# One-pass LayerNorms, four memory projections at each of four of them, and an output projection opened on seven heads

## The chip, the core and the metric

The kernel is one program on one core of a Trainium2 chip. It has a TensorE (PE, with PEld for its weight loads), a VectorE (DVE), a ScalarE (ACT), a GpSimd (POOL) and a SyncE (SP), which issues transfers. The metric is the device time of one execution in microseconds (us), as the median of several runs of the same kernel. Lower is better.

## What is computed

A two-layer decoder trunk is applied to 512 prompt tokens and to 32 sample tokens (8 sequences of 4), width 1024, all in float32. Each layer is a mixer, an attention over 256 memory tokens and a feed-forward part, and each of these three is added to the scaled stream and normalised:

```python
def _layer_norm(x, g, b):
    mu = jnp.mean(xf, axis=-1, keepdims=True)
    var = jnp.mean(jnp.square(xf - mu), axis=-1, keepdims=True)
    return ((xf - mu) * lax.rsqrt(var + LN_EPS) * g + b).astype(x.dtype)

for i in range(DEPTH):
    # layer 0: RG-LRU mixer; layer 1: gated delta rule
    x = _layer_norm(DN_ALPHA * x + mix, ...)                               # 0 and 3
    x = _layer_norm(DN_ALPHA * x + _mem_attention(x, mk, mv, wq, wo), ...) # 1 and 4
    # layer 0: SwiGLU; layer 1: 8 experts, 2 of them per token
    x = _layer_norm(DN_ALPHA * x + ff, ...)                                # 2 and 5
```

The numbers behind the lines are those by which the kernel counts its LayerNorms. The keys and values of the memory, `mem_prompt` times `xa_wk` and `xa_wv` of both layers, are outputs too; the sample tokens attend to cached ones. The delta rule has 8 heads of 128; each head's output is normalised by its root mean square, gated, and then all go through one output projection.

## The kernel before

**Layout.** Activations lie feature by feature: `x` is 128 partitions by 8 tiles (KT) by 544 tokens. A feature sum across partitions is therefore a product with a matrix of ones. For projections in front of the experts, each operand is split into a high and a low part (`xh` and `xl`, `wh` and `wl`), and a tile of output is 48 matmuls: high times high, low weight times high, high weight times low, 8 feature tiles and 2 halves of 272 tokens each (`lin_steps`, L537).

**Weights.** SP loads slots of 512 KB into a ring of 4 (`raw`, L389 to L437). POOL splits each into `wh` (L467) and `wl` (L471), each in four pieces. These have 2 places, so that POOL may split a slot only when the slot two before it has been used. PE reports a used slot on `w_used`, with the last of its 48 products. The 16 memory projections of each layer (`kv`, L584) need no split: they read `raw` and a copy of the memory `A_mem`; tiles 0 to 7 are keys (L600), 8 to 15 values (L604). Those of layer 1 are done within the LayerNorms 0 to 2, by `KV1_AT` (L23): 2 and 2 in the first, 3 and 5 in the second, 2 and 2 in the third. Their slots stand in the order of the slots between those of the projections on both sides. Layer 1's keys and values are stored to memory and loaded again after the delta rule, which uses the same place.

**A LayerNorm** (PE L567, ACT L1165, DVE L1641). While the projection before it runs, DVE evicts each tile (`residual`, L1659; L1666) and adds it to a running sum (L1656). Behind the last tile PE sums that over features (L570), DVE subtracts the mean from all eight tiles (L1644), ACT squares each of them (L1172) into one of two buffers, PE sums these over tiles and features (L577), ACT makes the reciprocal deviation (Ln L1177, Exp L1178), DVE multiplies eight tiles (L1647), ACT writes the eight high parts (L1182) and then the eight results (L1186), and DVE the low parts (L1633). The first part of the memory projections stands on PE's queue behind the first sum, the second behind the last one; ACT evicts each (L1141 to L1145), the second part between the results. In front of LayerNorm 2, DVE adds up the eight tiles only after the last of them (L1725).

**What follows each.** 0 and 3: the query projection of the attention (`linear`, L560), its first tile in the order of the feature tiles as they become ready; 1: the feed-forward part (`experts`, L692); 2: the delta rule's projections, begun with 30 products, then a small projection for its rates (L810); 4: the router (L1022), with three token transposes after its fourth feature tile (L1014), and then the routing. LayerNorm 5 is computed token by token in the branch taken here (L1147); `layer_norm(5)` is the other branch's.

**The end of the delta rule.** Head 7's output is evicted (`out_parts`), squared by ACT (L1413), summed by PE (`out_length`, L857, which waits for the sample state's `d_ssn`, L1909), scaled and gated (`out_norm`), and split into `hh` and `hl`. PE then waits for the eighth head's low part (L999), and the output projection, 8 tiles of 48, begins. ACT loads the keys and values back and fetches the first three pieces of cached keys (L1199) behind the last tile.

## Time and profile before

| | us |
|---|---|
| median of 3 runs | 2652.28 |
| lowest and highest run | 2652.21, 2659.44 |
| the profiled execution, its own time | 2667.02 |
| its span, first to last instruction | 2665.0 |

| engine | busy us | share of the span | instructions |
|---|---|---|---|
| PE | 2407.8 | 90% | 17290 |
| PEld | 2284.6 | 86% | 17290 |
| POOL | 961.3 | 36% | 1397 |
| DVE | 854.4 | 32% | 1423 |
| ACT | 536.4 | 20% | 1017 |

The mean granted TensorE clock of that execution is 0.931 of full speed. Busy time is an average over stages with different limits: a PE that is busy for 90% of the span still has gaps, and those are found by stage, with the chain of waits and the windows.

### The profile page before, as it was taken

What the parts mean: (1) busy time and instruction counts of PE and PEld (TensorE: products, weight loads), DVE (VectorE), ACT (ScalarE), POOL (GpSimd) and SP (SyncE); (2) the same over time, 40 slices, a digit from 0 to 9 for tenths busy, and PEclk for the clock granted to TensorE, in tenths of its full rate; (3) what the DMA queues carried; (4) which work ended last, traced back from release to release, by engine and by line L of the source; (5) the groups of instructions that cost most, each with busy time, mean ns of one, the idle gap of its engine ahead of it and who ended that gap; (6) DMA issues with size and microseconds to landing.
All of it is one profiled execution on the core that took longest, in us unless ns stands there. A gap on an engine that the chain in (4) does not pass through costs nothing.

```text
span 2665.0 us, 42930 instructions
## 1 busy us (share of the span) xinstructions
PE 2407.8 (90%) x17290; PEld 2284.6 (86%) x17290; DVE 854.4 (32%) x1423; ACT 536.4 (20%) x1017; POOL 961.3 (36%) x1397
## 2 busy tenths in 40 slices
PE   8998889999999987999999888889689999999993
PEld 8988858899999967899989777777579999999993
DVE  3673222211011037666666542412301000000004
ACT  2450320310011033333322211321200000100103
POOL 4546614588888725433322103544100000000001
PEclk9999999999999988999988777899789999999996
DMA  7314341322222221211111101341255677788884
GB/s 285 99 61 177 126 182 59 115 88 79 88 87 87 79 71 59 58 59 59 58 52 59 35 25 64 148 160 64 79 188 180 220 238 238 232 266 268 279 286 161
DMA packets 98376, 347.55 MB, mean 130 GB/s; under 512 B 13488, under 2 KB 18736, under 8 KB 93344
## 3 DMA queue, kind: packets, MB, share of 16 engines
q1 hardware_dynamic: 73136, 279.08, 31.2%
q10 hardware_dynamic: 19056, 44.65, 4.7%
q0 software_dynamic: 6016, 21.43, 2.2%
q8 instruction: 122, 2.00, 0.3%
q14 instruction: 46, 0.38, 0.0%
HBM read 318.66 MB, written 26.47 MB: 130 GB/s over the span
## 4 chain that ended last, share of the span: by engine, by line
PE 73%; DVE 10%; issue 7%; DMA 4%; ACT 3%; POOL 2%; ACTq 0%; DVEq 0%; SPq 0%; POOLq 0%
PE ps L548 29%; PE ps L1073 14%; PE ps L1088 8%; PE ps L727 6%; DMA raw<-weights 2%; PE ps L600 2%; PE ps L577 2%; PE ps L604 1%; PE ps L936 1%; PE ps L638 1%; PE ps L932 1%; DVE x L1647 1%; PE ps L915 1%; POOL wl L471 1%; PE ps L774 1%
## 5 line engine op out<-in xcount | busy, mean ns | idle before, releaser
L467 POOL TENSOR_TENSOR wh<-raw,tab 128x256 fp32r<-128x256 f32 x672 | 425.5, 664 | 940.7 <-PE ps L548 744.2
L471 POOL TENSOR_TENSOR wl<-raw,wh 128x256 fp32r<-128x256 f32 x672 | 507.3, 785 | 0.0
L1073 PE MATMUL ps<-work,raw 128*128 128x128 f32 (+6 forms) x3072 | 424.8, 300 | 13.4 <-DMA raw<-weights 11.0
L1073 PEld LDWEIGHTS ps<-work,raw 128*128 128x128 f32 x3072 | 420.5, 191 | 16.3 <-DVE work L2112 6.8
L548 PE MATMUL ps<-xh,wh 128*128 128x272 f32 x2048 | 309.8, 304 | 41.4 <-ACT work L1353 10.6
L548 PEld LDWEIGHTS ps<-xh,wh 128*128 128x128 f32 x2048 | 282.4, 199 | 50.8 <-issue 18.2
L548 PE MATMUL ps<-xh,wl 128*128 128x272 f32 x2048 | 296.8, 295 | 0.0
L548 PE MATMUL ps<-xl,wh 128*128 128x272 f32 x2048 | 281.8, 288 | 1.5 <-DVE xl L1633 1.4
L548 PEld LDWEIGHTS ps<-xh,wl 128*128 128x128 f32 x2048 | 275.3, 193 | 1.8 <-issue 0.5
L548 PEld LDWEIGHTS ps<-xl,wh 128*128 128x128 f32 x2048 | 265.5, 188 | 2.6 <-DVE xl L1633 2.6
L517 POOL DMA_DIRECT2D rows_y<-moe_h x8 | 4.3, 538 | 656.9 <-DVE moe_h L2105 656.9
L1088 PE MATMUL ps<-work,raw 128*128 128x128 f32 (+6 forms) x1536 | 218.0, 298 | 0.8 <-DVE work L2112 0.8
L1088 PEld LDWEIGHTS ps<-work,raw 128*128 128x128 f32 x1536 | 209.6, 190 | 1.6 <-DVE work L2112 1.4
L2112 DVE TENSOR_TENSOR work<-moe_h,ps 128x128 f32<-128x128 f32 (+6 forms) x96 | 30.6, 319 | 440.1 <-ACT moe_h L1563 440.1
L1563 ACT ACTIVATE moe_h<-ps 128x128 f32<-128x128 f32 (+6 forms) x96 | 29.0, 302 | 396.4 <-PE ps L1073 396.3
L1713 DVE TENSOR_TENSOR work<-work,ps 128x544 f32<-128x544 f32 x24 | 17.3, 721 | 225.8 <-PE ps L548 225.8
L2105 DVE COPY moe_h<-ps 128x256 f32<-128x256 f32 (+1 forms) x64 | 25.1, 391 | 197.2 <-PE ps L1061 155.6
L727 PE MATMUL ps<-hh,wh 128*128 128x272 f32 x384 | 81.4, 294 | 6.7 <-DVE hl L1633 6.7
L727 PE MATMUL ps<-hh,wl 128*128 128x272 f32 x384 | 80.4, 292 | 0.0
L727 PE MATMUL ps<-hl,wh 128*128 128x272 f32 x384 | 80.4, 292 | 0.0
L1172 ACT ACTIVATE lnsq<-x 128x544 f32<-128x544 f32 x40 | 26.3, 657 | 210.0 <-DVE x L1644 195.0
L1666 DVE SCALAR_TENSOR_TENSOR x<-x,ps 128x544 f32<-128x544 f32 x32 | 23.1, 721 | 139.9 <-PE ps L548 139.9
(358 smaller groups left out, 3121.3 us busy)
## 6 DMA issues: line engine op xcount, KB each, us to landing
raw<-weights SPq DMA_DIRECT2D x488, 512.0 KB, 3.9
moe_h<-cache SPq DMA_DIRECT2D x6, 2048.0 KB, 8.9
moe_h<-cache ACTq DMA_DIRECT2D x4, 2048.0 KB, 13.6
work<-cache SPq DMA_DIRECT2D x4, 2048.0 KB, 8.9
moe_h<-rows_x POOLq DMA_DIRECT2D x14, 512.0 KB, 7.8
rows_x<-lnsq ACTq DMA_DIRECT2D x9, 512.0 KB, 11.0
work<-scratch ACTq DMA_DIRECT2D x16, 272.0 KB, 4.2
work<-cache ACTq DMA_DIRECT2D x2, 2048.0 KB, 10.4
```

Source lines behind the costliest of these rows:

```text
L467: nc.gpsimd.tensor_tensor(flat(h1[:, k0:k1]), flat(r1[:, k0:k1]), one_col, MUL).then_inc(pool_hi, 1)
L471: low = nc.gpsimd.tensor_tensor(flat(l1[:, k0:k1]), flat(r1[:, k0:k1]), flat(h1[:, k0:k1]).bitcast(F), SUB)
L548: last = mm(ps[:, 2 * i + h, 0:HT], w[:, par_, k, :], a[:, k, h * HT:(h + 1) * HT], start=(n == 0 and k == 0), stop=(n == 2 and k == KT - 1))
L577: last = mm(ps[:, 6 + h, 0:HT], ones, lnsq[:, k % 2, h * HT:(h + 1) * HT], start=(k == 0), stop=(k == KT - 1))
L600: last = mm(ps[:, b, 0:MEM], raw[:, q, k, :], A_mem[:, k, :], start=(k == 0), stop=(k == KT - 1))
L604: last = mm(ps[:, b, mt * P:(mt + 1) * P], A_mem[:, k, mt * P:(mt + 1) * P], raw[:, q, k, :], start=(k == 0), stop=(k == KT - 1))
L638: last = mm(ps[:, 4 + tt // 2, (tt % 2) * MEM:(tt % 2 + 1) * MEM], A_q[:, 2 * h + kk, tt * P:(tt + 1) * P], A_k[:, 2 * h + kk, :], start=( ...
L727: last = mm(ps[:, 2 * d + h, 0:HT], w[:, s % 2, k, :], a[:, f, h * HT:(h + 1) * HT], start=(f == 0 and m == 0), stop=(f == FT - 1 and m == 2))
L1073: last = mm(ps[:, j // 2, (j % 2) * c:(j % 2 + 1) * c], raw[:, slot % RAW, k, :], M_x[:, r % 2, k, 0:c], start=(k == 0), stop=(k == KT - 1))
L1088: last = mm(ps[:, 2 + d % 2, 0:c], raw[:, slot % RAW, k, :], M_h[:, f, 0:c], start=(f == 0), stop=(f == FT - 1))
L1563: s(A(M_s[:, f % 2, 0:c], ps[:, f % 2, 0:c], ACT.Silu), m_silu, e12 + f + 1)
L2112: s(V.tensor_tensor(M_h[:, f, 0:c], M_s[:, f % 2, 0:c], ps[:, f % 2, c:2 * c], MUL), m_h, e12 + f + 1)
```

## The change

The LayerNorms 0 to 4 take the mean of the squares in place of the mean of squared differences. While a projection runs, ACT squares each evicted tile (`squares`) and DVE adds the square to a second running sum (`add_square`). Behind the last tile there are two sums over features, one next to the other; the variance is the second less the square of the first (`z_mean`), clipped at 0. DVE centres tile 0 before the variance and tile 1 after it, the other six each in front of its product with the deviation.

`KV1_AT` gives each of the LayerNorms 0 to 3 four projections of layer 1: one before the two sums, three behind them. ACT evicts the first behind the square of the mean and the others behind the first three high parts. The memory is loaded a second time for the last four, and of the values only the first half is loaded back. The first pieces of cached keys are fetched behind LayerNorms 0 and 3 instead of ahead of them.

Behind the LayerNorms 0, 1 and 3 PE does the high-part products of the first two tiles before the low-part products of either. In the output projection `opening` does all three parts of the first two tiles for the heads 0 to 6, and then the head 7 for both. The eighth head's sums no longer wait for the sample state and have other banks. The router's transposes stand behind its sixth feature tile instead of its fourth. In front of LayerNorm 2 the additions stand between the evictions. `layer_norm(5)` keeps its old form as `last_norm`.

```diff
-KV1_AT = {0: (0, 2, 4), 1: (4, 7, 12), 2: (12, 14, 16)}
+KV1_AT = {0: (0, 4), 1: (4, 8), 2: (8, 12), 3: (12, 16)}
...
             def linear(slot, direct, ah, al, freed, base, fresh=None, opened=False):
+                if fresh is not None:
+                    pairs = [lin_steps(slot + s, direct, s, s, ah, al, fresh=fresh, per=2 * KT) for s in range(2)]
+                    for steps in pairs:
+                        next(steps)
+                        next(steps)
+                    for steps in pairs:
+                        for _ in steps:
+                            pass
...
             def layer_norm(n):
+                if n in KV1_AT:
+                    lo, hi = KV1_AT[n]
...
+                    kv(1, lo, lo + 1)
+                pe.wait_ge(z_sum, n + 1)
+                for h in range(2):
+                    last = mm(ps[:, 6 + h, 0:HT], ones, lnsq[:, 0, h * HT:(h + 1) * HT], start=True, stop=True)
+                last.then_inc(ln_sum, 1)
+                pe.wait_ge(z_sq, n + 1)
+                for h in range(2):
+                    last = mm(ps[:, 4 + h, 0:HT], ones, lnsq[:, 1, h * HT:(h + 1) * HT], start=True, stop=True)
+                last.then_inc(ln_var, 1)
+                if n in KV1_AT:
+                    kv(1, lo + 1, hi)
+                    pe.wait_ge(kv_ev, 16 + hi)
...
+            def squares(n):
+                act.preload_act_table_set("natural_log_exp_and_others")
+                for t in range(KT):
...
+                    if t >= 2:
+                        act.wait_ge(z_acc, (KT - 2) * n + t - 1)
+                    s(A(lnr[:, :] if t else lnsq[:, 1, :], x[:, t, :], ACT.Square), z_pw, KT * n + t + 1)
...
             def layer_norm(n):
-                lo, mid, hi = KV1_AT[n] if n in KV1_AT else (0, 0, 0)
+                lo, hi = KV1_AT[n] if n in KV1_AT else (0, 0)
+                act.wait_ge(ln_sum, n + 1)
+                s(A(two(lnsq[:, 0, :]), pair(3), ACT.Square, scale=D ** -0.5), z_mean, n + 1)
+                if lo < hi:
+                    kv(1, lo)
+                act.wait_ge(z_var, n + 1)
+                s(A(lnr[:, :], lnr[:, :], ACT.Ln, bias=pc("eps5"), scale=1.0 / D))
+                s(A(lnr[:, :], lnr[:, :], ACT.Exp, scale=-0.5), ln_std, n + 1)
...
+                for k in range(KT):
+                    upper(n, k)
+                    if lo + 1 + k < hi:
+                        kv(1, lo + 1 + k)
+                for k in range(KT):
+                    result(n, k)
...
             def layer_norm(n):
+                dve.wait_ge(z_mean, n + 1)
+                centre(0)
+                dve.wait_ge(ln_var, n + 1)
+                s(V.tensor_tensor(two(lnr[:, :]), pair(2), two(lnsq[:, 0, :]), SUB))
+                s(V.tensor_scalar(lnr[:, :], lnr[:, :], 0.0, None, ALU.max), z_var, n + 1)
+                centre(1)
+                dve.wait_ge(ln_std, n + 1)
+                for k in range(KT):
+                    if k >= 2:
+                        centre(k)
+                    s(V.tensor_tensor(x[:, k, :], x[:, k, :], lnr[:, :], MUL), ln_n, n * KT + k + 1)
...
+            def add_square(t, n):
+                if t:
+                    dve.wait_ge(z_pw, KT * n + t + 1)
+                    add = V.tensor_tensor(lnsq[:, 1, :], lnsq[:, 1, :], lnr[:, :], ADD)
+                    s(add, *((z_acc, (KT - 2) * n + t) if t < KT - 1 else (z_sq, n + 1)))
...
             out_length(GH - 1)
-            pe.wait_ge(d_yl, GH)
             pe.wait_ge(d_z, GH)
-            linear(S_GOUT, 32, hh, hl, z_ready, KT * 2)
+            opening(S_GOUT, 28, hh, hl, range(GH - 1), (d_yh, d_yl))
+            linear(S_GOUT, 28, hh, hl, z_ready, KT * 2, opened=True)
```

## Rows read from the trace of the kernel before

**Rows 1.** The page: the chain that ended last, by line.

```profile
PE ps L548 29%; PE ps L1073 14%; PE ps L1088 8%; PE ps L727 6%; DMA raw<-weights 2%; PE ps L600 2%; PE ps L577 2%; PE ps L604 1%; PE ps L936 1%; PE ps L638 1%; PE ps L932 1%; DVE x L1647 1%; PE ps L915 1%; POOL wl L471 1%; PE ps L774 1%
```

**Rows 2.** The chain of waits, LayerNorm 0: start us, us, what.

```profile
261.33 1.19 PE ps L570 x4
262.52 6.91 PE ps L600 x32
269.42 7.88 PE ps L577 x32
...
277.39 0.72 ACT lnr L1177
...
278.13 0.67 ACT lnr L1178
...
287.74 0.85 ACT xh L1182
...
290.77 0.39 ACT work L1141
...
291.21 8.81 PE ps L548 x52
```

**Rows 3.** Windows, five LayerNorms: PE, PEld, DVE, ACT, POOL; clock, DMA share, GB/s.

```profile
259.70:291.20 31.50, 22.87 (x100) 18.42 (x100) 16.83 (x20) 17.86 (x26) 13.45 (x16) 0.96 0.61 234
454.60:500.00 45.40, 39.28 (x230) 34.64 (x229) 17.33 (x23) 20.90 (x32) 10.77 (x15) 0.96 0.25 82
946.10:984.40 38.30, 25.93 (x165) 23.00 (x164) 19.52 (x26) 16.57 (x25) 10.09 (x16) 0.88 0.25 82
1685.50:1704.00 18.50, 11.65 (x36) 8.00 (x36) 9.21 (x13) 8.77 (x13) 5.54 (x8) 0.82 0.97 395
1874.40:1890.20 15.80, 9.32 (x37) 6.18 (x37) 8.88 (x13) 7.48 (x12) 0.00 (x0) 0.99 0.00 0
```

**Rows 4.** Timeline, ends of five stages: start us, us, engine, line, operation.

```profile
305.67 2.33 POOL L467 TENSOR_TENSOR wh<-raw,tab 128x256 fp32r<-128x256 f32 x4 [0.90 <-PE ps L548]
...
512.13 2.18 PE L548 MATMUL ps<-xh,wh 128*128 128x272 f32 x16
...
990.27 7.51 PE L810 MATMUL ps<-x,par 128*8 128x272 f32 x64
...
1724.34 2.18 PE L548 MATMUL ps<-xh,wh 128*128 128x272 f32 x16
...
1908.94 0.19 DVE L2059 COPY work<-ps 128x32 f32<-128x32 f32 x1 [14.42 <-PE ps L1022]
```

**Rows 5.** Line L1656, additions: duration ns min/median/max.

```profile
L1656 DVE TENSOR_TENSOR lnsq<-lnsq,x x30: 724/986/1052, 230.2 to 1875.2; 128x544 f32<-128x544 f32 x30
```

**Rows 6.** Timeline: POOL's splits; output tiles 2 and 7.

```profile
299.67 2.33 POOL L467 TENSOR_TENSOR wh<-raw,tab 128x256 fp32r<-128x256 f32 x4 [12.61 <-PE ps L548]
301.95 2.81 POOL L471 TENSOR_TENSOR wl<-raw,wh 128x256 fp32r<-128x256 f32 x4
...
1647.64 2.23 PE L548 MATMUL ps<-hh,wh 128*128 128x272 f32 x16
...
1653.95 3.29 POOL L467 TENSOR_TENSOR wh<-raw,tab 128x256 fp32r<-128x256 f32 x4
...
1679.25 2.24 PE L548 MATMUL ps<-hh,wh 128*128 128x272 f32 x16 [0.27 <-POOL wl L471]
```

**Rows 7.** Timeline and window behind a gap of 2.55 us.

```profile
404.63 3.65 PE L548 MATMUL ps<-xh,wh 128*128 128x272 f32 x16 [2.55 <-issue]
...
404.60:408.00 3.40, 3.37 (x16) 3.40 (x17) 0.00 (x0) 0.00 (x0) 0.00 (x0) 0.56 0.00 0
```

**Rows 8.** Timeline: a value projection of the memory.

```profile
479.15 3.73 PE L604 MATMUL ps<-raw,work 128*128 128x128 f32 x32
```

**Rows 9.** Timeline: the sums for head 7's norm.

```profile
1624.76 2.15 PE L862 MATMUL ps<-lnsq,tab 128*128 128x272 f32 x4 [3.88 <-DVE work L1909]
```

**Rows 10.** Transfers: count, KB each, median us to landing.

```profile
moe_h<-cache ACTq DMA_DIRECT2D x4, 2048.0 KB, 13.6
```

More of the change, by code:

```diff
@@ L1723, in one @@
                           f_y, e8 + (d + 1))
-                repeat(dve, n, one, s)
-                for k in range(KT):
-                    add_tile(k, n_ln)
+                        if isinstance(e, int) and e + 1 == n:
+                            add_tile(d, n_ln)
+                            add_square(d, n_ln)
+                if gated:
+                    repeat(dve, n, one, s)
+                else:
+                    for e in range(n):
+                        one(e)
             def log1p_half(e, t0, t1, t2):
```

199 lines of the change are left out of this document (130 added, 69 removed).

## The prediction

> **What bounds the kernel now.** I read the page's chain by line first: its large shares are PE's products (L548 29%, L1073 14%, L1088 8%), a transfer holds 2% [rows 1]. Time is won where PE stands still, not by faster engines elsewhere. Next came the chain of waits around LayerNorm 0, for the order in which its steps end [rows 2]: the sum over features (1.19), two memory projections (6.91), a ping-pong of squares and their sums (7.88), Ln and Exp (0.72, 0.67), a DVE and ACT phase; the next projection starts at 291.21. PE's last product ended at 259.70, so the stage takes 31.5 us. Then the windows, one per LayerNorm, each from PE's last product to its next dense work [rows 3]: POOL is idle for more than half of every one. LayerNorm 5 lies in a branch that this input doesn't take (the chain runs through L1073 and L1088, in the other one [rows 1]).
>
> Last came the points where a stage really ends. POOL splits weights two slots ahead of PE, so a stage is over when the third tile behind it (tile 2) starts. Now that is, for LayerNorm 0, 305.6 (POOL's split at 305.67 waits for the same product), 45.9 after PE's last one; for 1: 512.13, 57.5; for 3: 1724.34, 38.8. Stage 2 ends with the small beta/rate projection, 990.27 + 7.51 = 997.8, 51.7; stage 4 with the logits copied out at 1908.94, 34.5 [rows 4].
>
> **The new LayerNorm, from PE's last product at 0.** A DVE step on a tile takes 0.72 and 0.03 to issue [rows 5]. DVE evicts tile 7 and adds it to the sum (0.1 + 2 x 0.72), ACT squares it beside that (0.67), DVE adds the square (0.72): sums complete at 1.6 and 2.4. In stages 0 to 3 one projection stands first in PE's queue (6.91 / 2 = 3.45), so the two cross-feature sums end at 4.6 and 5.6. ACT squares the mean (0.72): 5.4. DVE centres tile 0 (0.75), subtracts (0.72), clips. The trace has no such clip: at least half an addition, 0.36, at most a whole one, 0.72; I take 0.43. With Ln and Exp the reciprocal deviation is there at 8.9, against 278.8 - 259.7 = 19.1 now [rows 2].
>
> Part of that goes back, since six of eight centrings now stand behind the deviation. Additions of two tiles take 0.72 alone and up to 1.05 [rows 5], the latter while POOL splits, as it will here; a product with the deviation has the same form. 2 x 1.05, then 6 x (0.75 + 1.05 + 0.04) puts the last one at 22.1; high part 23.0 (0.85 and 0.02 each), eight results 30.0, last low part 30.8. The three other projections end with their evictions near 16 and hide under this; uncovered they would cost 3 x 3.45. PE's products of high parts trickle behind ACT until 23.3; then low weights 2.6, the second tile's 32 products 4.3, both tiles' low parts 4.4: 34.6. The two open tiles hold both slots, the first until 32.4. Only then can POOL start slot 2, 2.33 + 2.81 [rows 6]: tile 2 at 37.7.
>
> So PE waits 3.1 us, and that has its own price: behind 2.55 us without work the granted clock was 0.56, mostly the 1.2 GHz level, and 16 products took 3.65 [rows 7] against 2.18 in [rows 4]. With what the next 16 lose I count 1.65.
>
> Stage **0**: 45.9 - 37.7 - 1.65 = 6.5 won. **1**: four of its eight projections go to stage 3: 57.5 - 37.7 - 1.65 = 18.1 won. **2**: DVE no longer adds eight tiles behind the last eviction; projections are 3.73 each [rows 8] and PE waits 0.9 for tile 7 first; deviation at 9.9, high parts 24.0, 14 products at the low clock 2.9, the small projection 7.5: 34.7 instead of 51.7, 17.0 won. **3** takes up four projections (14.9) and can load weights only as they free slots; they end near 19 and still hide: 38.0 instead of 38.8, less the wait: 0.8 lost. **4**, without projections: deviation at 7.1, first result at 8.8 instead of 15.8; PE's router products and turns follow as now: 7.0 won.
>
> **The output projection.** Its first two tiles may start on seven heads once the sums for the eighth's norm are out. PE now waits 3.88 for them (until 1624.76, for the sample state's L1909) and they run at the low clock, four in 2.15 where [rows 2] has 1.19 [rows 9]. Without that wait they start near 1622.7. Behind them 42 products, the first 16 cold, 7.1; 42 more, 5.7; the eighth head. The first slot is free at 1638.5, and with a split of 5.65 tile 2 starts at 1644.1 instead of 1647.64 [rows 6]: 3.5, of which 1.5 goes for the cold start behind this new gap. At full clock it would be 5.6 in all, and 0 if the eighth norm were late; I take 2.0.
>
> **What the sums cost on the way.** Every evicted tile brings DVE one more addition with both operands in SBUF while POOL splits. Two of them stretch four POOL pieces from 2.33 to 3.29 [rows 6], 0.48 each. POOL's slot goes from 5.6 to 6.1 in three projections and from 6.1 to 6.6 in the fourth; PE's tile takes 6.0 (299.67 to 305.67). The fourth shows what 6.1 does: six tiles 6.32 apart, 1647.64 to 1679.25. So 18 x 0.27 = 4.9, and 6 x 0.28 = 1.7, 6.6 lost. Bounds: 0 if the additions fall where POOL idles; above, the first rival. In the feed-forward's down phase (under 0.7 per slot) POOL's idle 0.90 [rows 4] covers them; without it some 0.6 per slot.
>
> The queues: SP loads the same 488 slots, POOL skips the unsplit ones as now. ACT fetches 4 MB (layer 0) and 6 MB (layer 1) of cached keys after the LayerNorm instead of before, and reloads the memory (1 MB) beside the keys at the end of head 7, some 45 us before PE wants it. I cost these at 0: they land under eight query tiles of 6 us; uncovered, the last rival but one. ACT's new waits (each square for the addition before it) hold back nothing due, and DVE's wait for the square only the next eviction, due 6 us later.
>
> **Sum**: 6.5 + 18.1 + 17.0 - 0.8 + 7.0 + 2.0 - 6.6 = 43.2. The profiled execution lasted 2667.0 (span 2665.0 and 2.0 around it), 14.7 over the median; it would become 2624, and the median 2652.3 - 43.2 = 2609, which I predict.
>
> **Rivals.**
> *POOL becomes the bound of the projections.* In [rows 5, 6] both sides lose part of an addition (0.33, 0.48). If each addition stopped POOL for its whole 0.72, slots would be 6.6 in three projections and 7.3 in the fourth: 18 x 0.6 + 6 x 1.0 = 17 lost instead of 6.6: 2619. The Trainium skill (SBUF — State Buffer, "Who interferes with whom") states that rule: the later of two such operations blocks fully. By that rule this case should hold everywhere; the rows show less. 15%.
>
> *Evictions queue behind the high parts.* PE may not open before the last projection is evicted, and just such an eviction (0.39 at 290.77) released it at 291.21 [rows 2]. If the last comes behind the eighth high part instead of the third, PE begins 7 us later, cold, and does in a burst what would have trickled: 3 per stage, 12 in all: 2621. Against: 16 is well under 23. 10%.
>
> *No price for short waits.* Gaps that cost no clock and additions that fall into POOL's idle time: 3 x 1.65 + 1.5 + 6.6 = 13 more, 2596. Against: the 2.55 us row. 15%.
>
> *Slower: cached keys arrive late.* In layer 1 three fetches of 2 MB start some 31 us behind PE's last product instead of at once; the scores want them at about 80. ACT's fetches now land in 13.6 us [rows 10], three in a row 41, under the 49 there are. Above 16 us each PE stands; from (49 + 43) / 3 = 31 us each the gain is gone; at 36 the kernel takes 2668. For it: weights share the queues. Against: beside LayerNorm 3 the fetches moved at 395 GB/s [rows 3]. 4%.
>
> *It doesn't do what it says*: the shorter chains end in the same wait for POOL or low parts, and stages 1 and 2 keep half of their gain: 17.6 less, 2627. 4%.
>
> **How the numbers follow.** Forecast (2600 to 2618) 52%, the rivals as said. 2590 to 2626 leaves out the last two (8%) and the tails of the others; it takes in 0 to 17 for POOL, 0 to 5.6 for the opening, 0 to 6 for the gaps. 0.3% (8 us) is about what a measurement can tell from no change: faster than that in all but the slower case and some far tails: 0.93; same 0.03; slower 0.04.
>
> **What would show it.** Right: two groups of four sum products per LayerNorm; Ln some 7.5 us behind PE's last product (17.7 now); POOL's third split at 32 to 33, tile 2 at 37 to 40 in stages 0, 1 and 3; logits out near 27.5 in stage 4; six output tiles 6.6 apart. Wrong: tile 2 past 42, POOL's slots past 6.6, PE waiting for the cache, the small projection ending past 38. A result above 2644 would mean that the stages end elsewhere than I read them.

## The result and the profile after

The changed kernel takes 2637.25 us (2634.41 to 2642.49, 6 runs) where the kernel before takes 2659.20 (2652.21 to 2664.01) on the same chip: ratio 0.9912, 95% interval 0.9893 to 0.9932. A second series gave 2635.79 and 0.9901 (0.9884 to 0.9918). So it is faster, by 22 to 27 us, where 43.2 were forecast; the forecast ratio of 0.9836 (2609 over 2652.3) lies outside both intervals. The two profiled executions differ by as much: a span of 2639.3 now, 2665.0 before.

The page's chain by line still has PE's products in front ([rows 1]), but POOL's splits (L472, L468) now make up 5% of it, where the page before gives POOL 2%:

```profile
PE ps L550 25%; PE ps L1138 14%; PE ps L1153 8%; PE ps L788 4%; POOL wl L472 3%; DMA raw<-weights 3%; POOL wh L468 2%; PE ps L651 1%; DVE x L1762 1%; PE ps L1000 1%; PE ps L996 1%; PE ps L979 1%; PE ps L655 1%; PE ps L835 1%; DVE x L1750 1%
```

Stage by stage, from the two traces (PE's last product is the end of the projection ahead of a LayerNorm, or the start of the memory projection that now follows it at once, 0.16 us before that end; LOUT, O and GOUT are the recurrence's, the attention's and the delta rule's output projections):

| stretch | before | after | won | forecast |
|---|---|---|---|---|
| everything up to LOUT's first product | 208.8 | 206.9 | 1.9 | 0 |
| LayerNorm 0: last product to the scores of attention 0 | 82.6 | 85.0 | -2.4 | +6.5 |
| scores and outputs of attentions 0 and 1 | 125.1 | 129.5 | -4.4 | 0 |
| LOUT and O, O: first product to last | 151.0 | 154.0 | -3.0 | -4.9 |
| LayerNorm 1: last product to the first down phase | 193.5 | 178.2 | 15.3 | 18.1 |
| first down phase and second up phase | 224.5 | 222.9 | 1.5 | 0 |
| second down phase | 73.5 | 76.3 | -2.8 | 0 |
| LayerNorm 2: last product to the small projection's end | 51.7 | 35.5 | 16.2 | 17.0 |
| from there to GOUT's last product | 687.7 | 688.7 | -1.0 | +0.3 |
| LayerNorm 3: last product to the scores of attention 1 | 76.0 | 78.5 | -2.5 | -0.8 |
| LayerNorm 4: last product to the logits | 34.6 | 27.7 | 6.9 | 7.0 |
| from the logits to the end | 756.1 | 756.1 | 0 | 0 |
| sum | | | 25.7 | 43.2 |

In the column of what was won, a minus is time lost. The new LayerNorm does what its steps said. Here is PE behind LOUT, which ends at 258.10 (timeline of PE; start us, us, engine, line, operation, in brackets the idle time before and who ended it). [Rows 2] has the same stage before:

```profile
261.55 1.08 PE L613 MATMUL ps<-lnsq,tab 128*128 128x272 f32 x4
262.46 1.08 PE L617 MATMUL ps<-lnsq,tab 128*128 128x272 f32 x4
...
280.68 0.82 PE L550 MATMUL ps<-xh,wh 128*128 128x272 f32 x2 [0.69 <-ACT xh L1244]
281.30 3.80 PE L550 MATMUL ps<-xh,wl 128*128 128x272 f32 x16
...
288.95 4.16 PE L550 MATMUL ps<-xl,wh 128*128 128x272 f32 x32
303.88 3.99 PE L550 MATMUL ps<-xh,wh 128*128 128x272 f32 x16 [10.77 <-ACT work L1300]
```

The cross-feature sums end 4.5 and 5.4 us behind the last product (4.6 and 5.6 forecast), the eighth high part is there at 22.5 (23.0), and POOL's third split runs from 291.26 to 296.3, 33.2 to 38.2 behind (32.4 to 37.7). But the third query tile starts at 303.88, 45.8 behind instead of 37.7, after 10.77 us in which PE waited for ACT's line L1300, the eviction of query tile 0. The chain of waits says why (start us, us, what):

```profile
258.26 3.45 PE ps L651 x16
...
288.60 14.58 DMA out_mem_k<-work
...
303.88 38.49 PE ps L550 x288
```

ACT had issued two fetches of 2 MB of cached keys, then the store of four projected keys to `mem_k`, and then waited for that store, because the buffer `A_st` shares its bytes with the attention's `A_pt` (`act.wait_ge(out_done, 80)` ahead of `attention(0)`). The view of the transfers to `out_mem_k` has it with its price:

```profile
L1426 ACTq DMA_DIRECT2D out_mem_k<-work x1: 488/488/488, 288.6 to 288.6; - x1
...
  ACT work L1300: 15.6, 1
...
DMA to landing us min/median/max: 14.6/14.6/14.6
```

The two fetches landed 7.6 and 12.9 us behind their issue, the second at 301.0, and the store 2.2 us behind that (transfers of line L1295):

```profile
DMA to landing us min/median/max: 7.6/10.3/12.9
```

Before, ACT issued the fetches ahead of the LayerNorm; they had landed by 273.4 when the same store went out at 296.4, and it landed in 2.7 us (transfers to `out_mem_k` in the kernel before):

```profile
DMA to landing us min/median/max: 2.7/2.7/2.7
```

In the window in which it was under way now, 366 GB/s were moved, and PE's granted clock was 0.73 on average:

```profile
288.60:303.20 14.60, 4.51 (x37) 4.29 (x35) 1.76 (x1) 0.00 (x0) 10.07 (x16) 0.73 0.98 366
```

The other stages end as forecast, a little late. These lines answer to [rows 4] (timeline): the third tile of the feed-forward's first up phase, of the query projection behind LayerNorm 3, and the copy of the logits:

```profile
497.68 4.00 PE L550 MATMUL ps<-xh,wh 128*128 128x272 f32 x16 [3.75 <-POOL wl L472]
...
1698.82 3.96 PE L550 MATMUL ps<-xh,wh 128*128 128x272 f32 x16 [3.35 <-POOL wl L472]
...
1883.18 0.19 DVE L2197 COPY work<-ps 128x32 f32<-128x32 f32 x1 [9.86 <-PE ps L1086]
```

The third tiles start 39.2 and 38.9 us behind PE's last product (37.7 and 38.0 forecast), logits are out at 27.7 (27.5). Both tiles run cold, which in this text means at the lower of the clock's two levels, 1.2 GHz: the granted clock (the third number from the end) is 0.50 in the window of the first, as in that of the second.

```profile
497.68:501.68 4.00, 4.00 (x17) 4.00 (x18) 0.00 (x0) 0.00 (x0) 4.00 (x7) 0.50 0.41 131
```

### The profile page after: what moved, and what is told of

It is laid out like the page before. It is cut to its first block, busy times and chain, and to the rows that moved or that the text cites. A ratio compares the mean times of both kernels' runs of the same rounds, so it can differ in the third digit from the quotient of the medians.

```text
span 2639.3 us, 42728 instructions
## 1 busy us (share of the span) xinstructions
PE 2380.0 (90%) x17150; PEld 2264.9 (86%) x17150; DVE 898.8 (34%) x1468; ACT 540.3 (20%) x1022; POOL 985.0 (37%) x1397
## 4 chain that ended last, share of the span: by engine, by line
PE 63%; issue 15%; DVE 10%; POOL 5%; DMA 4%; ACT 3%; ACTq 0%; POOLq 0%; DVEq 0%; SPq 0%
PE ps L550 25%; PE ps L1138 14%; PE ps L1153 8%; PE ps L788 4%; POOL wl L472 3%; DMA raw<-weights 3%; POOL wh L468 2%; PE ps L651 1%; DVE x L1762 1%; PE ps L1000 1%; PE ps L996 1%; PE ps L979 1%; PE ps L655 1%; PE ps L835 1%; DVE x L1750 1%
## 5 line engine op out<-in xcount | busy, mean ns | idle before, releaser
L468 POOL TENSOR_TENSOR wh<-raw,tab 128x256 fp32r<-128x256 f32 x672 | 438.8, 684 | 898.0 <-PE ps L550 603.1
L472 POOL TENSOR_TENSOR wl<-raw,wh 128x256 fp32r<-128x256 f32 x672 | 518.6, 803 | 0.0
L1138 PE MATMUL ps<-work,raw 128*128 128x128 f32 (+6 forms) x3072 | 424.2, 299 | 13.2 <-DMA raw<-weights 10.8
L550 PEld LDWEIGHTS ps<-xh,wh 128*128 128x128 f32 x2048 | 284.3, 200 | 70.0 <-issue 20.8
L550 PE MATMUL ps<-xh,wl 128*128 128x272 f32 x2048 | 303.5, 299 | 0.0
L550 PEld LDWEIGHTS ps<-xh,wl 128*128 128x128 f32 x2048 | 281.7, 198 | 1.8 <-issue 0.5
L788 PEld LDWEIGHTS ps<-hh,wh 128*128 128x128 f32 x384 | 61.5, 193 | 8.7 <-issue 8.3
L1240 ACT ACTIVATE lnr<-x 128x544 f32<-128x544 f32 x35 | 23.1, 660 | 214.7 <-DVE x L1798 157.7
```

The costliest lines, as they stand in the source:

```text
L468: nc.gpsimd.tensor_tensor(flat(h1[:, k0:k1]), flat(r1[:, k0:k1]), one_col, MUL).then_inc(pool_hi, 1)
L472: low = nc.gpsimd.tensor_tensor(flat(l1[:, k0:k1]), flat(r1[:, k0:k1]), flat(h1[:, k0:k1]).bitcast(F), SUB)
L550: last = mm(ps[:, 2 * i + h, 0:HT], w[:, par_, k, :], a[:, k, h * HT:(h + 1) * HT], start=(n == 0 and k == 0), stop=(n == 2 and k == KT - 1))
L788: last = mm(ps[:, 2 * d + h, 0:HT], w[:, s % 2, k, :], a[:, f, h * HT:(h + 1) * HT], start=(f == 0 and m == 0), stop=(f == FT - 1 and m == 2))
L1138: last = mm(ps[:, j // 2, (j % 2) * c:(j % 2 + 1) * c], raw[:, slot % RAW, k, :], M_x[:, r % 2, k, 0:c], start=(k == 0), stop=(k == KT - 1))
```

## The experiments

All ratios are to the kernel before on the same chip.

**The store first.** In ACT's program:

```diff
+            act.dma_start(O["mem_k"][1][:, 0:4, :], A_st).then_inc(out_done, 16)
             act.wait_ge(w_used, S_LOUT + 8)
             piece(0, 1)
             piece(0, 2)
-            act.dma_start(O["mem_k"][1][:, 0:4, :], A_st).then_inc(out_done, 16)
             act.wait_ge(out_done, 80)
```

> The changed kernel with one move: behind LayerNorm 0, ACT issues the 0.5 MB store of four projected keys before the two 2 MB fetches of cached keys, not after them. Theory (the store waited behind 4 MB that the same queue had just been given): it lands in about 3 us instead of 14.58, ACT evicts query tile 0 at once, and the third query tile starts 38 us behind PE's last product, with POOL's third split, instead of 45.8: about 7.5 us won against the changed kernel, some 2630 us, ratio to before near 0.989. Rival (memory traffic of weights and keys slows any store at that place): it still takes over 10 us, the third tile starts past 43, no time is won. Second rival (the fetches, issued some 0.5 us later, then come late for the scores): PE waits several us more for cached keys near the fourth head (now 0.28) and gives the gain back there.

Measured: 2634.31 us, ratio 0.9892 (0.9877 to 0.9907). The store landed in 3.6 us, PE's wait is for POOL again, and the stretch from LOUT's last product to the scores is 77.65 us instead of 85.03 (transfers to `out_mem_k`, then PE's timeline):

```profile
DMA to landing us min/median/max: 3.6/3.6/3.6
...
298.45 3.58 PE L550 MATMUL ps<-xh,wh 128*128 128x272 f32 x16 [3.33 <-POOL wl L472]
```

The cached keys hardly came late: PE's wait for them in attention 0 is 0.7 us (0.3 in the changed kernel). The intervals of the two ratios (0.9892 here, 0.9912 for the change) overlap; that the stage is 7.4 us shorter is read from the traces.

**One fetch ahead of the store.** The store between `piece(0, 1)` and `piece(0, 2)`:

> The changed kernel with the same store between the two 2 MB fetches: one ahead of it, not two. Theory (it waits for the bytes ahead of it in ACT's queue): it lands in roughly half of 14.58, 7 to 9 us, near 296 us of the span, about when POOL has split the third weight slot (296.3), so PE's wait for ACT shrinks from 10.8 to 3 to 4 us, of which POOL's split is the end. Rival (memory traffic): near 14 us as with two ahead. Rival (a fixed price for any store behind any fetch): near 14 us too.

Measured (one run, 2627.39 us, beside 2663.73): the store landed in 10.5 us, PE waited 6.02 for ACT and the third tile started at 299.72.

```profile
DMA to landing us min/median/max: 10.5/10.5/10.5
...
299.72 3.59 PE L550 MATMUL ps<-xh,wh 128*128 128x272 f32 x16 [6.02 <-ACT work L1300]
```

So 3.6, 10.5 and 14.6 us with none, one and two fetches ahead of it (13.4 for two in a second run of the change): each 2 MB adds to the wait, the first more than the second, so that 10.5 is over the expected 7 to 9. The fetch ahead of the store explains the size: it landed in 8.3 us (the lowest value of its line), and the store 2.6 us behind it, about the 2.7 that the store takes alone.

```profile
DMA to landing us min/median/max: 8.3/11.9/15.6
```

Neither rival (14 us whatever stands ahead, or no change with the store first) survives. The Trainium skill (DMA: Bandwidth & Descriptors, "Queues, rings and completion order") says that each transfer engine consumes the descriptors of a ring in order and that a transfer's semaphore is raised only after the earlier writes of the same transfer engine; the three landings agree with that.

**One tile first.** The change interleaves the two first tiles of a projection behind a LayerNorm, as in the prediction. Here they run one after the other, in `linear` and in the experts' `up`:

```diff
-                if fresh is not None:
-                    pairs = [lin_steps(slot + s, direct, s, s, ah, al, fresh=fresh, per=2 * KT) for s in range(2)]
...
-                for s in range(2 if opened or fresh is not None else 0, 8):
+                for s in range(2 if opened else 0, 8):
...
-                    lin_tile(slot + s, direct, s % 2, s % 2, ah, al)
+                    lin_tile(slot + s, direct, s % 2, s % 2, ah, al, fresh=fresh if s == 0 else None)
```

> As the run with the store first, and in the three projections that follow LayerNorms 0, 1 and 3 the two first tiles are not interleaved: tile 0 runs through its three parts as the LayerNorm delivers them, then tile 1. Theory (POOL's third split waits for tile 0's slot, which the interleaving holds until tile 1's low weights are through): the slot is free when the last low part is (about 30.5 us behind PE's last product instead of 33.2), POOL's third split ends near 35.7, PE runs tile 1 (6 to 8 us) meanwhile and has no gap, and the third tile starts at 36.7 to 38.5 with PE at its high clock instead of at 38.2 to 39.1 at the low one: 1.5 to 4 us won in each of three stages, 4 to 12 in all against the run with the store first. Rival (the interleaving is what pays for the early start: without it 32 products of tile 1 that were hidden stand on the path): third tile at 40 or later, slower by 2 to 4 us per stage, 6 to 12 in all.

Measured: 2611.98 us, ratio 0.9805 (0.9790 to 0.9821). PE behind LOUT, whose last product ended at 259.4:

```profile
282.60 3.83 PE L550 MATMUL ps<-xh,wl 128*128 128x272 f32 x16
286.23 2.45 PE L550 MATMUL ps<-xl,wh 128*128 128x272 f32 x12
...
290.16 2.16 PE L550 MATMUL ps<-xh,wh 128*128 128x272 f32 x16
...
296.16 2.16 PE L550 MATMUL ps<-xh,wh 128*128 128x272 f32 x16
```

Tile 0 is done at 290.2, tile 1 runs without a stop while POOL splits, and the third tile starts at 296.16, 36.8 behind the last product, with no idle time and at 2.16 us for 16 products. The stretches to the scores or the down phase are 4.0, 4.8 and 3.8 us shorter than with the store first, at LayerNorms 0, 1 and 3. That is 12.5 of the 22 us between the two medians. Of the 20.8 us between the two profiled spans, 10.8 lie behind the logits, where nothing was changed (761.9 and 751.1 us): see "chance" below. The interleaving does not pay: the products that it does early are ones for which there is time anyway, since POOL cannot split before a slot is free.

**One tile first in the output projection.** `opening` finishes tile 0 (seven heads, then the eighth) before it starts tile 1:

```diff
-                    for n, (w, a) in enumerate(parts):
-                        for k in tiles:
...
-                rest = range(tiles[-1] + 1, KT)
-                for s in range(2):
-                    for n, (w, a) in enumerate(parts):
-                        for k in rest:
...
+                    for ks in (tiles, range(tiles[-1] + 1, KT)):
+                        for n, (w, a) in enumerate(parts):
+                            for k in ks:
```

> As the run with the store first, and the delta rule's output projection opens one tile after the other: tile 0 with seven heads and then with the eighth, only then tile 1, instead of both tiles with seven heads and then both with the eighth. Theory (opening both at once holds both weight slots, so that POOL's third split starts only at 1612.7 while the eighth head's low part had been there since 1606.4): POOL starts near 1607.5, the third tile near 1613.2 without PE's idle 6.45 and without the cold 16 products (3.64 instead of 2.18): 7 to 8 us won there, of which some goes back where POOL's slots stay 6.1 to 6.6 apart: 5 to 8 us against the run with the store first. Rival (the projection is bound by POOL's pace of 6.5 behind the opening whatever its start): under 2 us.

Measured: 2622.92 us, ratio 0.9836 (0.9822 to 0.9850). In the changed kernel (timeline of PE, then of POOL) the projection opens 1.6 us behind the sums at 1598.23, and POOL's third split waits until both tiles are through; the third tile starts 20.0 us behind the opening, after 6.45 idle:

```profile
1598.23 2.18 PE L926 MATMUL ps<-lnsq,tab 128*128 128x272 f32 x4 [2.06 <-ACT lnsq L1511]
1599.83 3.33 PE L570 MATMUL ps<-hh,wh 128*128 128x272 f32 x14
...
1619.85 3.64 PE L550 MATMUL ps<-hh,wh 128*128 128x272 f32 x16 [6.45 <-POOL wl L472]
...
1612.72 2.81 POOL L468 TENSOR_TENSOR wh<-raw,tab 128x256 fp32r<-128x256 f32 x4 [134.68 <-PE ps L579]
1615.49 4.21 POOL L472 TENSOR_TENSOR wl<-raw,wh 128x256 fp32r<-128x256 f32 x4
```

With tile 0 first (POOL's timeline, then PE's) the split starts 7.7 us behind the opening at 1594.17, the third tile 13.4 behind it, without a gap:

```profile
1601.84 2.81 POOL L468 TENSOR_TENSOR wh<-raw,tab 128x256 fp32r<-128x256 f32 x4 [129.46 <-PE ps L571]
...
1607.59 2.23 PE L550 MATMUL ps<-hh,wh 128*128 128x272 f32 x16
```

GOUT takes 56.1 us from its first product to the sums of LayerNorm 3, against 63.6 (7.5 won, at the top of the expected 5 to 8). The medians differ by 11.4 from the run with the store first, more than this stage gives.

**No opening.** PE waits for the eighth head's low part and then runs tile after tile:

```diff
-            opening(S_GOUT, 28, hh, hl, range(GH - 1), (d_yh, d_yl))
-            linear(S_GOUT, 28, hh, hl, z_ready, KT * 2, opened=True)
+            pe.wait_ge(d_yl, GH)
+            pe.wait_ge(d_ssn, GH)
+            linear(S_GOUT, 28, hh, hl, z_ready, KT * 2)
```

> The run with the store first, without the opening with seven heads: the delta rule's output projection starts when the eighth head's low part is there (about 8.2 us behind the sums for its norm), tile after tile, as before the change. Theory (both opened tiles held both slots, so the opening as it is won little): tile 0 starts near 8.3 us behind the sums' first product, cold, 8.2 us long, slot 0 is free at 16.5, POOL's third split ends at 22.2 and the third tile starts at 22.6 with PE at its high clock, against 21.6 with the opening, cold behind its gap of 6.45 (1.5 lost there): within 1 us of the run with the store first, slower or faster. Rival (the opening is worth the 2 us forecast or more): third tile 2 us or more later than with it after counting the cold start, 2 to 3.5 us slower.

Measured: 2627.86 us, ratio 0.9868 (0.9853 to 0.9884), no slower than with the opening. Tile 0 starts 8.3 behind the sums, the third tile 23.15, and from the sums to the last product's end it is 62.4 us, against 61.8 with the opening in the changed kernel and 62.6 in the trace of the store first: as the change has it, the opening is worth nothing that these traces can tell.

**The gap filled.** Products with ones that nobody reads, between the second and the third tile, in two lengths:

```diff
+            def keep_busy(n):
+                for i in range(n):
+                    mm(ps[:, 4, 0:HT], ones, lnsq[:, i % 2, 0:HT], start=True, stop=True)
...
+                    keep_busy(13)
```

> The run with the store first, with interleaved tiles as in the changed kernel, and between the second and the third tile behind LayerNorms 0, 1 and 3 PE multiplies 13 or 14 tiles of f32 by ones into a bank that nobody reads (0.23 us each at the high clock: 3.0 to 3.2 us, as long as its wait for POOL's third split). Theory (the low clock behind the gap comes from PE having stood still): the third tile starts where it did, 38 to 39 us behind PE's last product, but its first 16 products take 2.2 to 2.6 us instead of 3.6 to 4.0 and the next 16 2.2 instead of 2.6 to 3.2: 1.5 to 2.6 us won in each of three stages, 4.5 to 7.5 in all, ratio 0.986 to 0.9875. Rival (the low clock is a consequence of the trickle of products before, or of the burst's beginning, not of the gap): 16 products still take over 3.4 us and nothing is won.

Measured: 2629.02 us, ratio 0.9876 (0.9861 to 0.9891). I had taken one pass per product; the trace has two, so the filler lasted 6.1 us and the third tile came 2.4 us behind POOL's split, but at the high clock (granted 1.00, 2.4 GHz). Seven products instead:

> The run with the store first, tiles interleaved as in the changed kernel, and 7 products with ones (two passes of 0.23 us each, 3.2 us in all, where 13 had taken 6.1) in the gap before the third tile behind LayerNorms 0, 1 and 3. Theory (PE's low clock behind the gap is what the standstill costs, and nothing else waits): the third tile starts where it did without filler, 38.5 to 39.5 us behind PE's last product, its first 16 products take 2.2 to 2.4 us instead of 3.6 to 4.0, and the stretch from PE's last product to the scores becomes 1.5 to 2.5 us shorter in each stage (77.6 to about 75.5 for LayerNorm 0): 4.5 to 7.5 us in all, ratio 0.985 to 0.9865 beside 0.9873 to 0.9892. Rival (PE is bound by POOL's splits behind the gap in any case): the following tiles wait for POOL and the stretch keeps its 77.6.

Measured: 2623.66 us, ratio 0.9856 (0.9836 to 0.9876). The filler and the third tile (timeline of PE), the first fence with 13 products, the second with 7:

```profile
293.53 6.12 PE L589 MATMUL ps<-lnsq,tab 128*128 128x272 f32 x26
299.29 2.37 PE L550 MATMUL ps<-xh,wh 128*128 128x272 f32 x16
```

```profile
292.99 3.37 PE L589 MATMUL ps<-lnsq,tab 128*128 128x272 f32 x14
296.51 2.24 PE L550 MATMUL ps<-xh,wh 128*128 128x272 f32 x16
```

16 products behind the shorter filler take 2.24 us (4.00 and 3.96 behind the gaps of the changed kernel), at a granted clock of 1.00:

```profile
296.51:298.75 2.24, 2.24 (x18) 2.24 (x19) 0.00 (x0) 0.00 (x0) 2.24 (x5) 1.00 1.05 446
```

The three stretches are 2.2, 2.4 to 2.9 and 1.8 to 3.2 us shorter (75.39, 174.86 and, from the sums of LayerNorm 3 on, 72.21, where the two traces with the store first have 77.6, 177.3 to 177.7 and 74.0 to 75.4). Read at the third tile alone, its 48 products take 6.1 us behind the filler and 7.4 to 8.9 behind gaps of 3.3 to 3.8 us in the traces of the change and of the store first, where a tile without a gap takes 6.0. So a gap costs 1.4 to 2.9 us in these traces without any other wait.

**A doubled addition.** DVE adds twice behind each evicted tile:

```diff
-                    add = V.tensor_tensor(lnsq[:, 1, :], lnsq[:, 1, :], lnr[:, :], ADD)
+                    s(V.tensor_tensor(lnsq[:, 1, :], lnsq[:, 1, :], lnr[:, :], ADD))
+                    add = V.tensor_tensor(lnr[:, :], lnsq[:, 1, :], lnr[:, :], ADD)
```

> The run with the store first, and DVE makes one more addition of two SBUF tiles behind each evicted tile's addition of squares (its sum is overwritten), in the four projections and the last down phase. It prices the contention that the forecast took from before's rows. Theory (each addition stretches POOL's pieces by about 0.48 in sum, and where POOL sets the pace PE's tile is as much longer): POOL's slot in the attention's output projections goes from 6.1 to 6.6 and PE's tiles from 6.3 apart to 6.6 to 6.8, 2 to 2.5 us in each of two, as much in the two other projections, 1 to 3 us in the down phase: 9 to 13 us slower than the run with the store first, ratio 0.9926 to 0.994. Rival (each such addition stops POOL for its whole 0.72): tiles 6.9 to 7.0 apart, 15 to 20 us slower. Second rival (the additions fall where POOL idles): under 4 us.

Measured: 2640.04 us, ratio 0.9913 (0.9897 to 0.9928). POOL's slot in the attention's output projection (timeline) is two halves of 3.29:

```profile
429.33 3.29 POOL L468 TENSOR_TENSOR wh<-raw,tab 128x256 fp32r<-128x256 f32 x4
432.59 3.29 POOL L472 TENSOR_TENSOR wl<-raw,wh 128x256 fp32r<-128x256 f32 x4
```

That is 0.48 more than 3.29 and 2.82; PE's tiles are 6.62 apart instead of 6.32 there, and 6.99 instead of 6.52 in GOUT. The stretches add up to 8 to 10 us (1 to 2 in LOUT, 1.5 in each O, 3 to 4 in GOUT, 1 in the down phase); the ratios say 5.6 to 10.6, by which of the two series with the store first one takes. The price per addition is as forecast, and the rule of the rival (a whole 0.72) is out by the rows: tiles 6.62 apart, not 6.9 to 7.0. The Trainium skill (SBUF — State Buffer, "Summary: rules for kernel authors") has the later of two such operations blocked fully; here both sides lost a part, DVE's addition 0.30 (1.02 instead of 0.72) and POOL 0.48.

**The sums behind the down phase.** The additions for LayerNorm 2 in a loop of their own behind the eighth eviction:

```diff
-                        if isinstance(e, int) and e + 1 == n:
+                    if isinstance(e, int) and e + 1 == n:
+                        for d in range(KT):
                             add_tile(d, n_ln)
                             add_square(d, n_ln)
```

> The run with the store first, and the sums for LayerNorm 2 are made behind the last down phase's eighth tile, as before the change, not beside its evictions. Theory (beside POOL's splits they cost the down phase; behind it they stand on the path): the last down phase takes 73.5 to 74.5 us instead of 76.3, and the sums end 11 us behind PE's last product instead of 2.4, so that the stretch from there to the small projection's end is 8 to 10 us longer: 5 to 7.5 us slower in all, ratio 0.990 to 0.9915. Rival (the down phase grew by PE's clock at its start and not by the sums): it still takes over 75.5, 8 to 10 us slower, ratio 0.991 to 0.9925.

Measured: 2639.30 us, ratio 0.9906 (0.9888 to 0.9925). The chain of waits has the down phase whole again, 74.7 us instead of 76.3, and the sums at 939.77, 11.9 behind it:

```profile
853.15 74.68 PE ps L788 x576
...
939.77 2.18 PE ps L613 x4
```

The value lies between the two theories, and both hold: the sums cost the down phase 1.6 us; 1.2 of its growth remain without them, and these are PE's clock. In the phase's first 10 us the granted clock was 0.83 before and 0.70 here, and PE did 58 products instead of 68 (windows, the kernel before and this run):

```profile
872.63:882.63 10.00, 10.00 (x68) 10.00 (x69) 0.00 (x0) 0.00 (x0) 4.30 (x8) 0.83 0.17 52
853.15:863.15 10.00, 10.00 (x58) 10.00 (x59) 0.00 (x0) 0.00 (x0) 3.13 (x6) 0.70 0.18 54
```

This part comes and goes between traces: with the sums in place the phase takes 75.0 to 76.4 us. From the down phase's start to the small projection's it is 6.5 us longer, so the sums are well placed beside the evictions.

**Both orders.** Store first, one tile first everywhere:

> The store first, one tile after the other behind LayerNorms 0, 1 and 3, and one tile after the other in the opening of the delta rule's output projection, together. Theory (each order removes a wait of PE for POOL of its own, in different stages): the gains add. Against the run with the store first (ratio 0.9892) the first order won 0.0087 and the second 0.0056, so 0.975 (0.972 to 0.978), some 2597 us where before takes 2664. Rival (part of the first order's 23 us was chance: its tiles account for 14 of them in its trace, and waits for expert weights differ by up to 7 us between runs): 0.977 to 0.980.

Measured: 2611.32 us, ratio 0.9805 (0.9792 to 0.9818), no better than without the order in GOUT, and outside the expected 0.972 to 0.978, though the trace has all stretches short (73.7, 172.7, 56.1 and, from the sums of LayerNorm 3 on, 70.3). So that series was run again, beside the change and the store first:

> The changed kernel as it is, on the same chip and beside the same runs of before as the three below, since the order of the store (some 7 us in its stage) and the two orders of the tiles moved the time by amounts near the spread between executions. Theory (stages account for the time; expert weights and the scores add up to some 7 us of chance): 0.990 to 0.993 of before, as first measured (0.9912). Rival (the first measurement was lucky or unlucky by more): outside 0.988 to 0.995.

> The run with the store first once more, beside the changed kernel. Theory (the stage's 7.5 us arrive at the end): 0.0020 to 0.0036 below the changed kernel's ratio of the same chip, 0.987 to 0.989. Rival (cached keys or later waits take it back): within 0.0015 of it.

> Store first and both orders of the tiles once more. By its trace's stages it should lie 14 + 7.5 us below the run with the store first: 0.979 to 0.9805 if that is at 0.9875; the first two measurements gave 0.0087 between them. Rival (what the output projection won there is lost again in attention 1 by a mechanism, not by chance): the trace shows the scores of attention 1 at 66 us again (63 to 65 elsewhere) and more than 4 us of PE's wait for cached keys.

Measured: 0.9901 (0.9884 to 0.9918), 0.9873 (0.9851 to 0.9896), 0.9799 (0.9782 to 0.9815). The store is worth 0.0028 here and 0.0020 in the first series, 5 to 7.5 us. In the second trace of the change the store landed in 13.4 us and the stage took 83.5 (77.6 with the store first). Between the store first and both orders, on one chip, the medians differ by 18.6 us, near the 20 that the stretches give (12.5 and 7.5); why the first series shows only the gain of the first order is not shown. The rival of the third run needed two things: the scores of attention 1 did take 65.6 us again, but PE's wait for cached keys is 0.5 us there, not over 4.

**Chance** is why single differences of 5 us can't be read from these times. The same instructions took, in the traces of this study, 632.2 or 636.1 us (the delta rule's heads, in two executions of one and the same kernel), 62.7 to 66.7 (the scores of one attention), and PE waited 7.4 to 14.3 us for expert weights. The scores show where it comes from: in one attention PE's 389 products lasted 49.5 us at a mean granted clock of 0.97, 51.3 at 0.95 and 52.7 at 0.92, and the second and third line are the same kernel (windows of attention 0: before, the change, the change again).

```profile
342.29:404.63 62.34, 49.48 (x389) 30.37 (x389) 17.44 (x21) 20.22 (x46) 4.48 (x7) 0.97 0.48 186
343.13:407.19 64.06, 51.31 (x389) 31.75 (x389) 17.43 (x21) 20.25 (x46) 4.50 (x7) 0.95 0.47 181
342.15:407.58 65.43, 52.74 (x389) 32.87 (x389) 17.43 (x21) 20.22 (x46) 4.48 (x7) 0.92 0.46 177
```

The stretches of the stages repeat better, within 0.1 to 1.5 us.

**Results between the high parts.** From the traces, ACT's eight results in a row (6.96 us) hold up the low parts. Here result k-3 follows high part k:

```diff
                 for k in range(KT):
                     upper(n, k)
...
-                for k in range(KT):
+                    if k >= 3:
+                        result(n, k - 3)
+                for k in range(KT - 3, KT):
                     result(n, k)
```

> As the run before it (store first, both orders), and ACT writes the LayerNorm's result of tile k-3 behind the high part of tile k, not all eight results behind the eighth high part, in LayerNorms 0 to 3. Theory (the low parts, and so the first weight slot, wait for ACT's eight results, 6.96 us in a row, while ACT had idled 3.8 us between the high parts): five results fall into these gaps, the last result comes 3.3 us earlier, tile 0 ends 2.5 to 3.3 us earlier behind LayerNorms 0, 1 and 3, and the small projection behind LayerNorm 2 3.3 us earlier: 9 to 12 us against the run before it. Rival (the results delay the high parts and DVE's products by as much, ACT being as full as DVE there): the eighth high part ends past 24 us behind PE's last product (22.5 now), and less than 4 us are won.

Measured: 2612.11 us, ratio 0.9806 (0.9791 to 0.9822): nothing won, as the rival had it. In LayerNorm 2 it cost: the small projection ended 37.8 us behind the down phase instead of 35.0. The last low part came 28.5 us behind the last product instead of 30.3, but the eighth high part at 24.2, and behind it 16 cold products with low weights stood in PE's queue ahead of the low parts (timeline; the last product ended at 259.67):

```profile
283.89 0.82 PE L550 MATMUL ps<-xh,wh 128*128 128x272 f32 x2 [0.92 <-ACT xh L1221]
284.51 3.66 PE L550 MATMUL ps<-xh,wl 128*128 128x272 f32 x16
288.01 2.17 PE L550 MATMUL ps<-xl,wh 128*128 128x272 f32 x16
290.02 2.17 PE L550 MATMUL ps<-xh,wh 128*128 128x272 f32 x16
```

**Low weights between.** So PE takes each high part by high and by low weights as it comes, in the first tile:

```diff
+                for k in range(KT):
+                    pe.wait_ge(ln_xh, fresh + k + 1)
+                    for n, w in enumerate((wh, wl)):
+                        for h in range(2):
+                            mm(ps[:, h, 0:HT], w[:, 0, k, :], ah[:, k, h * HT:(h + 1) * HT],
+                               start=(n == 0 and k == 0), stop=False)
```

> Store first, both orders, results between the high parts in LayerNorms 0, 1 and 3 (in LayerNorm 2 as in the change), and in the first tile behind these three LayerNorms PE multiplies each high part by high and low weights as it comes, not all high weights first. Theory (with the results moved up, 16 cold products of 3.7 us behind the eighth high part took the place of the low parts as what ends tile 0): tile 0 ends 28.8 to 29.3 us behind PE's last product instead of 30.4 to 30.8, and the stretches to the next stage become 1.3 to 1.8 us shorter each: 4 to 6 us against the run with both orders (0.9799 to 0.9805), ratio 0.978 to 0.979. Rival (POOL's third split or tile 1 sets the third tile's start whatever tile 0 does): no stretch is shorter by over 0.5.

Measured: 2602.76 us (2599.87 to 2609.92), ratio 0.9790 (0.9773 to 0.9807), the fastest of the study: 57 us under the kernel before, about 30 under the change. Tile 0 ends at 287.72, 28.9 behind the last product (258.82):

```profile
283.66 0.66 PE L582 MATMUL ps<-xh,wl 128*128 128x272 f32 x2
284.11 3.77 PE L587 MATMUL ps<-xl,wh 128*128 128x272 f32 x16
287.72 2.16 PE L550 MATMUL ps<-xh,wh 128*128 128x272 f32 x16
```

The three stretches are 71.8, 170.7 and, from the sums of LayerNorm 3 on, 68.8, 1.5 to 2.0 shorter each than with both orders.

## Why the prediction was wrong

The sign, the mechanism and most of the terms were right; the time was 17 to 20 us too low, past the range. By its own steps:

- **The step that failed outright is the sentence on the queues**: "ACT fetches 4 MB (layer 0) and 6 MB (layer 1) of cached keys after the LayerNorm instead of before ... I cost these at 0". It looked at who wants the keys, and not at what stands behind the fetches in ACT's own queue: the store of projected keys, for which ACT waits before it evicts the first query tile. Stage 0 should have won 6.5 and lost 2.4. With the store first the stage wins 4.9 and the whole kernel 5 to 7.5 us, and the landing follows the bytes ahead of it (3.6, 10.5, 14.6). This is shown. It is not the whole miss: with the store first the ratio is 0.9873 and 0.9892, still above the forecast 0.9836. In layer 1 the same sentence cost about 1 us, PE's wait for cached keys (1.53 instead of 0.53).
- **The gap's price** was mis-sized: 1.65 us counted for each of three gaps; the third tile takes 2.3, 2.7 and 2.8 us more behind them in the trace of the change, 1.4 to 2.9 in those of the store first. The low weights behind the trickle were taken at 2.6 and took 3.80 (281.30), cold; with that the first slot was free 0.8 later, and the third tiles started 0.9 to 1.5 late. Stage 0 (with the store first) and stages 1 and 3 (in the change) fell short by 1.6, 2.8 and 1.7 us, about what these two add up to.
- **The order of the tiles** is no error of the sum: it was taken over from the change and its 3.1 us of PE's wait priced, not questioned. The prediction had the cause in one sentence, "The two open tiles hold both slots", and the runs show what it costs: 12.5 us in three stages and 7.5 in the output projection.
- **The output projection**: 2.0 forecast for the opening, nothing found by taking it out. The third tile came 21.6 us behind the sums, as forecast (21.4), though by another way (the slot free earlier, the split 7.0 us long instead of 5.65, since DVE evicts two tiles at once beside it). But without the opening it comes at 23.15 and at the high clock, which is as good. The earlier sums, 2.1 of the forecast, can't be found in the total: PE's wait in front of them fell from 3.88 ([rows 9]) to 2.06, but from the small projection's end to them it is 626.9 us as before (627.0), in heads that vary by 4.
- **The sums on the way**: 6.6 forecast, of which 4.9 for LOUT and the two O; they took 3.0, and GOUT's last tiles are 6.5 apart (6.6 forecast). The price of 0.48 per addition held when the additions were doubled. But "In the feed-forward's down phase ... POOL's idle 0.90 covers them" did not hold: 1.6 us by the run that takes them out; the other 1.2 of the 2.8 that the phase lost are the clock at its start.
- **Stages 2 and 4** were right: 16.2 for 17.0, 6.9 for 7.0. So was the new LayerNorm's chain, each step within 0.5 us up to the eighth high part.
- **The scores** took 4.4 us longer in the two attentions together, without a change to them: 3.5 of it PE's products at a lower clock (see "chance"), 0.9 the wait for cached keys. Across the traces of this study they take 62.7 to 66.7, and the kernel before, with one trace, 62.3 and 62.8; whether its clock there was luck or the change lowers it was not tried.

Of the rivals, none came true as told. "No price for short waits" is refuted by the filler, "POOL becomes the bound" by the doubled additions, "Evictions queue behind the high parts" and "cached keys arrive late" by the traces (the last projection is evicted at 274.0, 15.9 behind LOUT, and PE waits 0.3 and 1.5 us for keys), "It doesn't do what it says" by the 15.3 and 16.2 us won in stages 1 and 2. The one that happened, a moved fetch that delays a store behind which an eviction waits, was not among them, though the prediction's milestone "Wrong: tile 2 past 42" would have found it.

## What to carry to other kernels

When a transfer is moved, list what its issuing engine issues behind it and which waits hang on that: here a store of 0.5 MB behind 4 MB landed 2.2 us after the 4 MB, and the engine that waits for it may hold the next stage's evictions. Where weights come through two slots, as here, finish the first tile before the second is opened; products done early in a second open tile cost the slot that the third one needs. And when a wait is shortened, look for the next one in the same queue before counting the gain (results moved up won nothing until the low weights moved too).

## What was not expected of the hardware

A store of 0.5 MB landed in 3.6, 10.5 or 14.6 us by what stood ahead of it in ACT's queue. A short standstill of PE of 3.3 to 3.8 us cost 1.4 to 2.9 us in the 48 products behind it, although PE had run at the high clock up to it (a granted clock of 1.00 in the 6.2 us ahead of the gap behind LayerNorm 1 in the changed kernel, 0.50 behind it). One and the same kernel ran through the eight delta-rule heads in 632.2 or 636.1 us from one execution to the next (the store first, at a mean granted clock of 0.88 and 0.87).
